# Reordering the gated-delta recurrence and the first tile's output path in a hybrid attention and expert-retrieval kernel

## The chip, the cores and the metric

The kernel runs on one core of a Trainium2 chip. A time is the device time of one execution in microseconds. Three timed runs of the kernel before took 1912.2, 1913.64 and 1914.07 us, with a median of 1913.64.

## What is computed

One decoder layer is applied to 512 prompt tokens and to 8 sample tokens, all in float32. Cut to what matters here, it is:

```python
h = rmsnorm(x, g_pre_mix) * (1 + sc1) + sh1
proj = h @ w_in                    # attention q, k, v; conv input; decay, beta; z; gates g_a, g_b
o_att = sliding_window_attention(q, k, v)
# gated delta rule, in chunks, per head (DK = DV = 128)
tmat = inverse(I + lmat)           # lmat strictly lower triangular in a chunk
u, w = tmat @ (v * beta), tmat @ (k * beta * exp(g))
for each chunk:
    v_new = u_i - w_i @ S
    o     = (q_i * exp(g_i)) @ S + a_i @ v_new
    S     = S * exp(g_last) + (k_i * exp(g_last - g_i)).T @ v_new
o_d = rmsnorm(o, delta_norm) * silu(z)
merged = sigmoid(g_a) * (o_att @ w_att_out) + sigmoid(g_b) * (o_d @ w_delta_out)
x = x + gt1 * rmsnorm(merged @ w_out, g_post_mix)
h2 = rmsnorm(x, g_pre_ffn) * (1 + sc2) + sh2
# expert retrieval, 8 heads: the best 16 of 128 keys on both halves, the best 16 of their 256 sums
f = sum over (head, e) of softmax(best)[e] * gelu(h2 . expert_u[idx[e]]) * expert_v[idx[e]]
x = x + gt2 * rmsnorm(f, g_post_ffn)
```

The new caches and states are outputs too.

## The kernel before

The program is written by hand for five queues: PE (`tensor`), DVE (`vector`), ACT (`scalar`), GpSimd (`gpsimd`) and SP (`sync`, which issues most DMAs). Each runs its instructions in the order in which they are written, and waits on semaphores. Nothing reorders them, so this order is the schedule.

Tokens are tiled by 128: tiles 0 to 3 are the prompt and tile 4 holds the 8 samples. The recurrence is chunked by 128 too, so chunk 0 is tile 0. Four heads side by side make a product of four 128x128 matmuls into one PSUM bank of 512 columns.

The stages are the projections and attention (to about 350 us), the triangular inverse (to about 456 us), the recurrence with tile 0's way to its experts (to about 522 us), and the expert stage (the rest). The inverse is built by doubling: levels 1 to 6 each make, for the four chunks, a first product (`Lm`, `Wc`), copied to `A2` by ACT, and a second product (`A2`, `Tc`), subtracted by DVE. Level 6 writes `Wc`, the transposed inverse, and counts `wt_ready`.

The expert stage makes 520 gathers. GpSimd's `indirect_dma_start` (L446) fetches 128 rows of 8 KB of `euv`, an expert's u and v side by side, into a ring of 7 slots (`SLOTS`). DVE multiplies u with the replicated h2 and sums (L2086), ACT takes gelu and scales a pattern (L800, L804), PE sums the v parts (L1412) and frees the slot. The other tiles' projections, norms, queries and searches are woven between the ticks by tables. Slots 0, 1, 4, 5 and 6 lie over the convolution's outputs `ct`, slot 3 over `Wc`.

PSUM has 8 banks. `dring` (4 banks, `dbank`) goes from PE to DVE and `aring` (2 banks, `abank`) from PE to ACT: `to_fill` waits until a bank was freed, `to_read` until it was filled. `fsum` (2 banks) holds sums in the early and the last stage.

The names in the recurrence are these. On PE, `new_values(ch)` makes the product with `Wc`, `carried(ch)` the state's and the output's products from the new values, `state_products(ch)` the products of the state `delta` with keys and queries, `outputs(ch)` transposes the normed output, `first_deltas(half)` multiplies it with `w_delta_out` for tile 0, `mix(0, e)` makes a quarter (256 columns) of tile 0's `merged @ w_out`, `turned(0)` transposes h2, `first_query` and `first_scores` make the queries and key scores, `select(0)` the gather's indices. `sample_state(h)` with DVE's `state(h)` and `state_sum(h)` updates the samples' states, one head each. On DVE, `asked(ch)` makes the right side of the new values, `decayed(ch)` decays output and state, `carried()` adds what PE made, `squares()` and `normed(ch)` norm the output with ACT's `root_o(ch)`, `gated(ch)` multiplies by the gate; `search(0, piece)` finds the best keys of head 0. ACT's `mixed(0, e)` copies a quarter, `part_squares` sums its squares.

## Time and profile before

| What | Value |
|---|---|
| Median of the three timed runs | 1913.64 us |
| The profiled execution's own time | 1913.76 us |
| Its span | 1911.9 us |
| PE busy | 1452.9 us (76%) |
| DVE busy | 1249.1 us (65%) |
| ACT busy | 674.3 us (35%) |
| GpSimd busy | 620.9 us (32%) |
| DMA, all queues | 645.40 MB, mean 338 GB/s |
| Software queue q0 (the gathers) | 555.82 MB, 70.4% of 16 engines' span |
| Chain that ended last: DMA, PE, DVE, ACT | 39%, 37%, 10%, 6% |

A busy share is a mean over stages with different limits. The page's row of DMA shares is 3 or 4 tenths through most of the first quarter and 9 tenths from the twelfth of 40 slices to the last. In the timelines below, a row has the start in us, the duration in us, the engine, the line, the operation with its output and inputs, the count of instructions run together, and in brackets the idle time before with what ended it. A 128-column product in float32 counts as two PE instructions there, so x8 is one product over four heads. In the windows a pair is busy us with the count in brackets, and PEclk is the granted clock as a share of 2.4 GHz.

### The profile page before, as it was taken

Reading aid. Unit: us, or ns where it says so; the run is one execution under the profiler, and the core shown is the slowest. Engines: PE = TensorE matmul, PEld = TensorE weight load, DVE = VectorE, ACT = ScalarE, POOL = GpSimd, SP = SyncE. Lnnn points to the kernel's source line nnn. Section 1 sums busy time; section 2 is a strip of 40 time slices with the busy share of each in tenths; the row PEclk is TensorE's granted clock in tenths of the full one; section 3 lists DMA queues with packets and bytes.
Section 4 is the critical chain, followed back from the end, with each engine's and each line's share of the span. In section 5 each row is a group of like instructions: output and inputs, shape, how many; then the busy total and the mean of one; then the engine's idle time right before and its main releaser. Section 6 shows DMA issues by size and latency. Waiting matters only on the chain.

```text
span 1911.9 us, 22867 instructions
## 1 busy us (share of the span) xinstructions
PE 1452.9 (76%) x7696; PEld 680.8 (36%) x7696; DVE 1249.1 (65%) x2815; ACT 674.3 (35%) x1745; POOL 620.9 (32%) x590
## 2 busy tenths in 40 slices
PE   9999899999888879587877666666666666666565
PEld 4777678888734446133323111110110110000000
DVE  2077644787576655957767777676776667776765
ACT  3145544411344443723423232342332233322223
POOL 1100000000033424354444544444345444444442
PEclk9999999899999989689888766776676676666766
DMA  9533344103499999999999999999999999999997
GB/s 357 155 126 107 114 132 135 59 32 142 155 367 422 421 410 422 416 384 423 416 421 415 424 424 424 424 424 424 422 422 421 422 415 405 424 424 419 421 422 310
DMA packets 100452, 645.40 MB, mean 338 GB/s; under 512 B 11778, under 2 KB 11930, under 8 KB 32325
## 3 DMA queue, kind: packets, MB, share of 16 engines
q0 software_dynamic: 76912, 555.82, 70.4%
q1 hardware_dynamic: 23232, 88.04, 12.6%
q8 instruction: 61, 1.00, 0.2%
q14 instruction: 55, 0.45, 0.1%
q10 hardware_dynamic: 192, 0.09, 0.0%
HBM read 638.73 MB, written 6.18 MB: 337 GB/s over the span
## 4 chain that ended last, share of the span: by engine, by line
DMA 39%; PE 37%; DVE 10%; ACT 6%; issue 6%; POOL 1%; another core or an unknown queue 1%; DVEq 0%; ACTq 0%; SPq 0%; POOLq 0%
DMA arena<-in_euv,consts 38%; PE abank L831 21%; PE dbank L831 4%; PE dbank L1412 4%; DVE arena L2086 4%; PE fsum L1412 4%; ACT consts L804 1%; PE abank L1323 1%; ACT arena L463 1%; POOL arena L446 1%; ACT small L800 1%; DMA arena<-in_wstream 1%; PE abank L1336 1%; DVE arena L2008 1%
## 5 line engine op out<-in xcount | busy, mean ns | idle before, releaser
L2086 DVE CUSTOM_DVE_ANT_0 arena<-arena 128x1024 f32<-128x1024 f32 x520 | 634.0, 1224 | 408.5 <-DMA arena<-in_euv,consts 402.3
L446 POOL DMA_INDIRECT arena<-in_euv,consts x520 | 589.2, 1133 | 767.0 <-PE fsum L1412 378.3
L831 PE MATMUL abank<-arena 128*128 128x256 f32 (+4 forms) x2400 | 537.4, 383 | 18.5 <-ACT arena L463 9.2
L1412 PE MATMUL dbank<-arena,consts 128*32 128x512 f32 x1024 | 351.3, 860 | 218.5 <-ACT consts L804 217.5
L831 PEld LDWEIGHTS abank<-arena 128*128 128x128 f32 (+1 forms) x2400 | 400.1, 193 | 171.1 <-issue 70.8
L1412 PE MATMUL fsum<-arena,consts 128*32 128x512 f32 x1024 | 298.8, 781 | 182.8 <-ACT consts L804 180.8
L800 ACT ACTIVATE small<-small 128x1 f32<-128x1 f32 x520 | 104.8, 202 | 693.9 <-DVE small L2086 686.9
L1412 PEld LDWEIGHTS dbank<-arena,consts 128*32 128x32 f32 x1024 | 41.6, 126 | 492.3 <-ACT consts L804 482.2
L463 ACT ACTIVATE arena<-abank 128x512 f32<-128x512 f32 (+5 forms) x228 | 111.4, 488 | 288.6 <-PE abank L831 268.2
L1412 PEld LDWEIGHTS fsum<-arena,consts 128*32 128x32 f32 x1024 | 37.9, 120 | 391.4 <-ACT consts L804 375.2
L804 ACT ACTIVATE consts<-arena,small 128x32 f32<-128x32 f32 x520 | 167.1, 321 | 17.3 <-ACT small L800 0.3
L831 PE MATMUL dbank<-arena 128*128 128x128 f32 (+6 forms) x624 | 94.7, 323 | 0.7 <-ACTq L633 0.7
L831 PEld LDWEIGHTS dbank<-arena 128*128 128x128 f32 (+2 forms) x624 | 81.7, 198 | 12.0 <-issue 5.9
L800 ACT ACT_TABLE_LOAD x50 | 64.2, 1283 | 3.6 <-DVE small L2086 2.1
L427 POOL DMA_DIRECT2D out_deltas<-arena x1 | 0.5, 537 | 158.4 <-DVEq L1743 158.4
L1637 DVE RECIPROCAL arena<-arena 128x520 f32<-128x520 f32 x8 | 27.2, 3403 | 37.2 <-ACTq L559 37.2
L463 ACT ACT_TABLE_LOAD x34 | 43.6, 1283 | 7.3 <-PE abank L831 5.2
L1608 DVE COPY arena<-arena 128x24 f32<-128x24 f32 x12 | 2.2, 180 | 64.6 <-ACTq L527 64.4
L2086 DVE DVE_READ_ACCUMULATOR2_ANT small<- 128x1 f32 x520 | 42.8, 82 | 0.0
L713 ACT ACT_TABLE_LOAD x32 | 41.1, 1283 | 1.3
L463 ACT ACTIVATE consts<-abank 128x32 f32<-128x32 f32 (+1 forms) x33 | 6.5, 197 | 96.7 <-PE abank L1323 63.3
L1336 PE MATMUL abank<-arena,consts 128*32 128x512 f32 x256 | 37.0, 636 | 1.2 <-ACT consts L463 1.2
(305 smaller groups left out, 1128.8 us busy)
## 6 DMA issues: line engine op xcount, KB each, us to landing
arena<-in_wstream SPq DMA_DIRECT2D x132, 512.0 KB, 4.6
arena<-in_euv,consts POOLq DMA_INDIRECT x520
arena<-in_wout SPq DMA_DIRECT2D x8, 1024.0 KB, 10.3
arena<-mod SPq DMA_DIRECT2D x7, 512.0 KB, 13.4
arena<-in_x SPq DMA_DIRECT2D x5, 512.0 KB, 7.1
arena<-in_sdel POOLq DMA_DIRECT2D x1, 2048.0 KB, 8.3
out_deltas<-arena POOLq DMA_DIRECT2D x1, 2048.0 KB, 7.5
out_yp<-arena SPq DMA_DIRECT2D x4, 512.0 KB
```

What stands on the lines that cost most here:

```text
L446: pool.indirect_dma_start(ring[n % SLOTS], None, I["euv"], bass.IndirectOffsetOnAxis(cur[:, u % 2, c:c + 1], 0)).then_inc(ring_in[n % SLOT ...
L463: step(A(dst, src, func, **kw), s.aring_free)
L713: A(gexp[r, :], best[r, :], ACT.Exp, bias=nbest[r, :], accum_out=gsum[r, :]).then_inc(s.gexp_ready, 1)
L800: step(A(gel[:, q % 2, place:place + 1], dot[:, q % 2, place:place + 1], ACT.Gelu), s.gelu_done)
L804: A(S[:, q % 2, place, :], E4g[:, u % 2, c0:c0 + 32], ACT.Copy, scale=gel[:, q % 2, place:place + 1]).then_inc(s.diag_ready, 1)
L831: return pe.matmul(out, lhsT, rhs, start=first, stop=last)
L1323: last = pe.matmul(b[32 * k:32 * k + 32, 8 * j:8 * j + 8], ident[:, 32 * j:32 * j + 32], pick[:, :, 4 * k:4 * k + 4], start=True, stop=Tru ...
L1336: last = pe.matmul(b[32 * k:32 * k + 32, :], ident[:, 32 * j:32 * j + 32], h2_all[t][:, g * 512:(g + 1) * 512], start=True, stop=True, ski ...
L1412: last = pe.matmul(out[e][to:to + 32, :], weighed, v, start=h == 0 and kk == 0, stop=h == PH - 1 and kk == 3, skip_group_check=True)
L1637: step(recip(r, r))
L2008: did(0, TT(hit[r], hit[r], bc(sif[r], 2, TOPK), ALU.mult))
L2086: TTR(uh, uh, rep[j] if t < NT else h2sb, 1.0, 0.0, ALU.mult, ALU.add, dot[:, n // NQ % 2, n % NQ:n % NQ + 1]).then_inc(s.dots_done, 1)
```

## The change

The sixth level is taken out of the level loop, in products per chunk, and woven into the recurrence: chunk 0 goes through it first, and the new values of a chunk wait for that chunk's `wt_ready` alone. For chunk 0 the output's product goes to `fsum[0]`, is squared and scaled from there, and its transposition goes to `fsum[1]`; `first_deltas` uses the two `fsum` banks in place of `dring` banks. `state_products` is split in `key_products` and `query_products`. The mix quarters follow each other with less between them, and their weights are requested one by one, each when its place is free, in other places. In the norms the factor rows are multiplied in ahead of the reciprocal root (`gained`, and the products in `first_second`), so that one operation follows it. `warm(3)` makes three products of which nothing is used. The last chunk's recurrence goes behind `search(0, ...)` on DVE and behind `select(0)` on PE; the gather that waits for `o_ready` is now number 3.

PE, from the sixth level of chunk 0 on (`fsum`, `abank`, `dbank` are PSUM banks). Before:

```order
L831 MATMUL abank0<-arena 128x128 x4
L831 MATMUL abank1<-arena 128x128 x4
L831 MATMUL abank0<-arena 128x128 x4
L831 MATMUL abank1<-arena 128x128 x4
L831 MATMUL dbank0<-arena 128x512
L831 MATMUL dbank1<-arena 128x512
L831 MATMUL dbank2<-arena 128x128 x4
L831 MATMUL dbank3<-arena 128x128 x4
L831 MATMUL dbank0<-arena 128x128 x4
L831 MATMUL dbank1<-arena 128x128 x4
L831 MATMUL abank0<-arena 128x128 x4
```

And now, to the transposition of the output:

```order
L840 MATMUL abank0<-arena 128x128 x4
L840 MATMUL abank1<-arena 128x128 x4
L840 MATMUL dbank0<-arena 128x128 x4
L840 MATMUL abank0<-arena 128x128 x4
L840 MATMUL abank1<-arena 128x128 x4
L840 MATMUL abank0<-arena 128x128 x4
L840 MATMUL dbank1<-arena 128x128 x4
L840 MATMUL fsum0<-arena 128x128 x4
L840 MATMUL dbank2<-delta,arena 128x128 x4
L840 MATMUL dbank3<-arena 128x128 x4
L840 MATMUL abank1<-delta,arena 128x128 x4
L1203 MATMUL fsum1<-consts,arena 128x128 x4
```

Chunk 0's new values are the eleventh row before and the fifth now. `sample_state(2)`, the two rows of 512 columns, went behind this stretch.

PE, from the second half of `first_deltas` to the last mix quarter. Before (the first two rows are `carried(1)`, the `delta` rows the state products, L1025 a transposition, the last x4 row `new_values(2)`):

```order
L831 MATMUL dbank1<-arena 128x128 x4
L831 MATMUL dbank2<-arena 128x128 x4
L831 MATMUL dbank3<-arena 128x128 x16
L831 MATMUL dbank0<-delta,arena 128x128 x4
L831 MATMUL abank1<-delta,arena 128x128 x4
L831 MATMUL abank0<-arena 128x256 x8
L831 MATMUL abank1<-arena 128x256 x8
L1025 MATMUL dbank1<-consts,arena 128x128 x4
L831 MATMUL abank0<-arena 128x256 x8
L831 MATMUL abank1<-arena 128x128 x4
L831 MATMUL abank0<-arena 128x256 x8
```

And now (two second products and the new values of chunk 1 first; the rows of 512 columns are `sample_state(3)`):

```order
L840 MATMUL fsum1<-arena 128x128 x16
L840 MATMUL dbank2<-arena 128x128 x4
L840 MATMUL dbank3<-arena 128x128 x4
L840 MATMUL abank0<-arena 128x128 x4
L840 MATMUL abank1<-arena 128x256 x8
L840 MATMUL dbank0<-arena 128x512
L840 MATMUL dbank1<-arena 128x512
L840 MATMUL abank0<-arena 128x256 x8
L840 MATMUL abank1<-arena 128x256 x8
L840 MATMUL dbank2<-arena 128x128 x4
L840 MATMUL dbank3<-arena 128x128 x4
L840 MATMUL abank0<-arena 128x256 x8
```

The state products of chunk 2 and the transposition of output 1 went behind the last quarter.

DVE, ahead of tile 0's first norm (its reciprocal, L1849 before and L1900 now). Before, with `asked(2)`, `gated(1)` and `decayed(2)`:

```order
L1884 TENSOR_TENSOR arena<-dbank,small 128x512
L1885 TENSOR_TENSOR arena<-arena 128x512
L1830 SCALAR_TENSOR_TENSOR arena<-dbank,cols,arena 128x4x128
L1890 TENSOR_TENSOR arena<-arena,small 128x512
L1891 TENSOR_TENSOR delta<-delta,small 128x512
L1849 RECIPROCAL small<-small 128x1
```

And now:

```order
L1912 TENSOR_TENSOR arena<-arena 128x256
L1940 TENSOR_TENSOR arena<-dbank,small 128x512
L1941 TENSOR_TENSOR arena<-arena 128x512
L1912 TENSOR_TENSOR arena<-arena 128x256
L1900 RECIPROCAL small<-small 128x1
L1907 SCALAR_TENSOR_TENSOR arena<-arena,small 128x512 x2
```

`asked(2)` (L1940, L1941) stands between the last two parts of `gained` (L1912), directly ahead of the norm; `gated(1)` and `decayed(2)` went behind both norms.

The diff, cut to its core:

```diff
-                    if n == 4:
+                    if n == 3:
                         pool.wait_ge(s.o_ready, NT)
...
@@ ACT @@
+            first_product(0)
+            first_product(1)
+            first_product(2)
             new_values()
+            first_product(3)
+            act.wait_ge(s.fd_full, 1)
+            step(A(E1[:, 0, :], fsum[0][:, :], ACT.Square), s.psq_ready)
             root_o(0)
             carried_query()
             new_values()
-            root_o(1)
-            carried_query()
...
                 if e == 2:
-                    new_values()
+                    root_o(1)
             root_of(3, parts4[:, 2:3])
+            carried_query()
...
             root_of(5, parts4[:, 4:5])
-            carried_query()
-            root_o(2)
+            new_values()
...
@@ PE @@
+            def warm(times):
+
+                for _ in range(times):
+                    pe.matmul(fsum[0][:, :], ident, consts[:, 0:512], start=True, stop=True)
...
+            first_product(6, 0)
+            first_product(6, 1)
+            second_product(6, 0)
+            first_product(6, 2)
             new_values(0)
+            first_product(6, 3)
             carried(0)
-            sample_state(3)
-            pe.wait_ge(s.wt_ready, NT * 7)
-            state_products(1)
+            key_products(1)
+            second_product(6, 1)
+            query_products(1)
             outputs(0)
+            sample_state(2)
+            first_deltas(0)
+            first_deltas(1)
+            second_product(6, 2)
+            second_product(6, 3)
             new_values(1)
-            first_deltas(0)
-            carried(1)
-            first_deltas(1)
-            state_products(2)
             pe.wait_ge(s.merged0_ready, 1)
             mix(0, 0)
+            sample_state(3)
             mix(0, 1)
+            mix(0, 2)
+            carried(1)
+            mix(0, 3)
+            key_products(2)
+            query_products(2)
             outputs(1)
-            mix(0, 2)
             new_values(2)
-            mix(0, 3)
-            carried(2)
-            state_products(3)
+            warm(3)
...
             turned(0)
+            carried(2)
             pe.wait_ge(s.h2T_ready, 1)
             pe.wait_ge(s.skt_in, 16)
...
+            first_query()
+            first_query()
+            first_scores(0)
+            key_products(3)
+            query_products(3)
+            outputs(2)
+            first_query()
+            first_query()
+            first_scores(1)
+            first_query()
+            first_query()
+            select(0)
+            new_values(3)
+            carried(3)
...
@@ SP @@
-            sp.wait_ge(s.wt_ready, NT * 7)
-            for e in range(3):
-                first_quarter(e)
+            sp.wait_ge(s.lm_ready, NT * 7)
+            first_quarter(0)
             sp.wait_ge(s.mg_ready, NT)
             sp.wait_ge(s.E_ready, NT)
             sp.dma_start(x_t[:, 0, :], I["x"][0:P, :]).then_inc(s.xr0_in, 16)
-            sp.wait_ge(s.sd_ready, 1)
-            for i, v in enumerate(v_first):
-                sp.dma_start(v, bass.AP(tensor=I["mod"].tensor, offset=i * D, ap=[[0, P], [1, D]])).then_inc(s.mod_in, 16)
+            sp.wait_ge(s.a2_ready, NT * 6)
+            first_quarter(1)
+            sp.wait_ge(s.wt_ready, NT * 7)
+            first_quarter(2)
+            sp.dma_start(v_first[0], bass.AP(tensor=I["mod"].tensor, offset=0, ap=[[0, P], [1, D]])).then_inc(s.g1_in, 16)
             sp.wait_ge(s.mx_ready, 1)
             first_quarter(3)
+            sp.wait_ge(s.sd_ready, 1)
+            for i in (1, 2):
+                sp.dma_start(v_first[i], bass.AP(tensor=I["mod"].tensor, offset=i * D, ap=[[0, P], [1, D]])).then_inc(s.mod_in, 16)
...
@@ DVE @@
+            def last_merge(ch):
+
+                b = dring.to_read()
+                step(TT(Wc[:, ch, :], Wc[:, ch, :], b[:, :], ALU.subtract), s.dring_free)
+                dve.sem_inc(s.wt_ready, 1)
...
                 for half in (slice(0, 512), slice(512, D)):
-                    step(STT(h[:, half], h[:, half], rstd[:, 0:1], g1[:, half], ALU.mult, ALU.mult))
-                    step(TT(x_t[:, 0, half], x_t[:, 0, half], h[:, half], ALU.add), s.xs_ready)
+                    step(STT(x_t[:, 0, half], h[:, half], rstd[:, 0:1], x_t[:, 0, half], ALU.mult, ALU.add), s.xs_ready)
+
+            def gained(e):
+                h, g1 = h2_all[0][:, 256 * e:256 * e + 256], v_first[0][:, 256 * e:256 * e + 256]
+                dve.wait_ge(s.psq_ready, e + 2)
+                step(TT(h, h, g1, ALU.mult))
...
+            last_merge(0)
             b = dring.to_read()
             step(copy(delta[:, :], b[:, :]), s.dring_free)
             dve.sem_inc(s.S_ready, 1)
-            b = dring.to_read()
-            step(copy(o, b[:, :]), s.dring_free)
-            squares()
+            dve.wait_ge(s.psq_ready, 1)
+            step(dve.tensor_reduce(rms4, three(R), AX.X, ALU.add), s.o_ready)
+            dve.wait_ge(s.orms_ready, 1)
+            step(recip(rms4, rms4))
+            step(TT(three(o), three(fsum[0][:, :]), bc(rms4, 2, P), ALU.mult), s.on_ready)
+            gated(0)
+            asked(1)
+            last_merge(1)
+            state_sum(2)
+            first_deltas(0)
+            state(3)
+            first_deltas(1)
+            last_merge(2)
+            last_merge(3)
+            decayed(1)
             state_sum(3)
...
             for piece in range(5):
                 search(0, piece)
+            asked(3)
+            gated(2)
+            decayed(3)
             carried()
             squares()
```

## Rows read from the trace of the kernel before

**Rows 1.** Windows: us, busy PE, PEld, DVE, ACT, POOL; PEclk, DMA share, GB/s
```profile
524.00:545.00 21.00, 15.08 (x112) 7.92 (x104) 15.02 (x46) 9.70 (x21) 8.53 (x8) 1.00 1.01 405
545.00:560.00 15.00, 12.61 (x90) 5.47 (x83) 12.06 (x36) 7.19 (x17) 4.64 (x5) 0.89 0.73 251
560.00:1895.00 1335.00, 925.70 (x4348) 271.07 (x4346) 914.54 (x2196) 471.73 (x1371) 587.28 (x539) 0.77 1.01 419
```

**Rows 2.** Timeline of GpSimd: start, us, engine, line, operation, idle before
```profile
522.33 1.03 POOL L446 DMA_INDIRECT arena<-in_euv,consts  x1 [0.28 <-POOL consts L435]
```

**Rows 3.** Timeline of PE, level six to the delta projection
```profile
442.67 2.98 PE L831 MATMUL abank<-arena 128*128 128x128 f32 x24
...
446.98 5.75 PE L831 MATMUL dbank<-arena 8*128 8x512 f32 x36
...
453.29 1.16 PE L831 MATMUL abank<-arena 128*128 128x128 f32 x8 [0.56 <-DVEq L1821]
...
459.07 1.16 PE L831 MATMUL dbank<-delta,arena 128*128 128x128 f32 x8
...
461.95 0.66 PE L1025 MATMUL dbank<-consts,arena 128*128 128x128 f32 x4 [0.83 <-DVE arena L1907]
...
464.40 10.73 PE L831 MATMUL dbank<-arena 128*128 128x128 f32 x80
```

**Rows 4.** Timeline of PE, mixes to select
```profile
476.75 7.12 PE L831 MATMUL abank<-arena 128*128 128x256 f32 x32
...
497.65 1.30 PE L831 MATMUL dbank<-delta,arena 128*128 128x128 f32 x8 [3.75 <-DVEq L1896]
...
504.73 3.24 PE L831 MATMUL abank<-arena 128*128 128x128 f32 x16 [2.30 <-ACTq L692]
...
516.30 4.67 PE L831 MATMUL abank<-arena 128*128 128x128 f32 x40
...
521.03 0.44 PE L1323 MATMUL abank<-arena,consts 128*32 128x8 f32 x32
```

**Rows 5.** Timeline of DVE, level six to the end of the search
```profile
445.18 0.64 DVE L1684 STREAM_TRANSPOSE arena<-arena 32x128 f32<-32x128 f32 x2
...
452.49 3.19 DVE L1820 TENSOR_TENSOR arena<-arena,dbank 128x512 f32<-128x512 f32 x4
...
463.38 0.75 DVE L1830 SCALAR_TENSOR_TENSOR arena<-dbank,cols,arena 128x512 f32<-128x512 f32 x1
...
493.62 0.17 DVE L1849 RECIPROCAL small<-small 128x1 f32<-128x1 f32 x1 [6.88 <-ACT small L653]
...
496.12 0.69 DVE L1857 TENSOR_TENSOR arena<-arena 128x512 f32<-128x512 f32 x1
...
500.90 0.69 DVE L1864 TENSOR_TENSOR arena<-arena 128x512 f32<-128x512 f32 x1
...
512.33 0.49 DVE L1953 MAX8 arena<-arena 128x8 f32<-128x128 f32 x2 [1.09 <-ACTq L776]
...
520.75 0.23 DVE L2018 TENSOR_SCALAR arena<-arena 128x16 f32<-128x16 f32 x1
```

**Rows 6.** Timeline of ACT, same stretch
```profile
454.49 0.60 ACT L463 ACTIVATE arena<-abank 128x512 f32<-128x512 f32 x1 [6.80 <-PE abank L831]
...
459.44 0.30 ACT L637 ACTIVATE small<-small 128x4 f32<-128x4 f32 x1 [4.36 <-DVE small L1902]
...
492.15 0.38 ACT L463 ACTIVATE arena<-abank 128x256 f32<-128x256 f32 x1 [2.32 <-PE abank L831]
```

**Rows 7.** Windows as in rows 1, where the granted clock (PEclk) fell
```profile
465.00:470.00 5.00, 5.00 (x35) 5.00 (x34) 0.82 (x2) 0.23 (x1) 0.00 (x0) 0.72 0.95 330
...
500.00:502.00 2.00, 1.86 (x10) 1.46 (x9) 1.90 (x4) 0.60 (x1) 0.00 (x0) 0.51 0.01 4
...
506.00:508.00 2.00, 2.00 (x12) 2.00 (x11) 0.00 (x0) 0.00 (x0) 0.00 (x0) 0.50 0.04 8
```

**Rows 8.** Issues of DMAs from 440 to 530 us: count, KB, us to landing
```profile
arena<-in_wout SPq DMA_DIRECT2D x4, 1024.0 KB, 8.9
```

194 lines of the change are left out of this document (96 added, 98 removed).

## The prediction

> **What bounds the kernel now.** I read the windows first. From 560 to 1895 us the DMA share is 1.01 and 419 GB/s move, without a break [rows 1]: the 520 gathers of the last stage (L446) keep all DMA engines full. Only their beginning has a hole: 524 to 545 us is full, but 545 to 560 us has a share of 0.73, so 15 x (1.01 - 0.73)/1.01 = 4.2 us are lost there [rows 1]. The bytes are the same after the change, so the end comes as much earlier as the first gather does, and GpSimd's row dates it: 522.33 us [rows 2].
>
> What sets 522.33? I followed it back through the rows of PE, DVE and ACT. Index cast after PE's `select(0)` at 521.03 [rows 4], this after the search of head 0 on DVE (512.33 to 520.98) [rows 5], this after two queries (from 504.73) [rows 4], h2 (DVE, to 501.59), the first norm (from 493.62) [rows 5], the last mix quarter (copied at 492.15) [rows 6], the mixes (from 476.75) [rows 4], the first delta projection (from 464.40), chunk 0's new values (PE, 453.29) [rows 3]. That is the path of token tile 0; whatever else stands in the queues between is filler.
>
> **The change, step by step.** Up to the fifth level's merges nothing is moved, so I start from the same times: first products from 442.67, three in 2.98 us, 0.99 each [rows 3], last transposes on DVE done at 445.82 [rows 5]. Semaphore hops are 0.05 to 0.15 us where nothing stands between (ACT starts 0.04 us after PE's 453.29 + 1.16) [rows 3, 6]. I take 0.1.
>
> 1. *Chunk 0 alone through level six.* Before, the new values wait behind four first products, `sample_state(2)` and four second products (446.98, 5.75 us) and DVE's sums [rows 3]. Now: first products 0 and 1 end at 444.65, second product 0 at 445.65, first product 2 at 446.65. `last_merge(0)`, 0.7 us on DVE after 445.82 (four merges took 3.19 us [rows 5], so 0.7 to 0.8 each), ends at 446.6. New values at 446.75: 6.5 us earlier.
> 2. *Output read from PSUM.* New values 1.0, ACT's copy 0.60 [rows 6], so 448.55; PE is in first product 3 until 448.85; carried key product and output product 2.0 (a group of four 128-column products is 1.0: 1.16 for the first [rows 3]), 450.85; ACT squares 0.6, DVE reduces 0.7, root 0.30 [rows 6], reciprocal and scaling 0.9, transposes 0.66 [rows 3]. `gated(0)` starts at 454.7 instead of 463.38 [rows 5]: 8.65 earlier. It loses a copy and a product on DVE, and `state_sum(3)`, `asked(1)` from in front of it. Reading PSUM from ACT costs what ACT's reading of `abank` costs; I take 0.60, bounds 0.4 and 0.8 (the 128x256 and 128x512 rows are 0.38 and 0.60 [rows 6]).
> 3. *Delta projection.* PE has `sample_state(2)` first (two products of 512 columns, 5.75 less four groups of 1.0 = 1.7), so it starts at 456.25 instead of 464.40 [rows 3]: 8.15. Its last weight block (512 KB) is requested at its first product and needed 5.9 us later. The only row near is twice that size, 8.9 us to landing behind others in the queue [rows 8]; half of it is 4.5 and fits, all of it is 3 too much. I take no wait, bounds 0 and 3.
> 4. *To the last mix quarter.* PE work from there, before: 10.73 (two halves and `carried(1)`), 2 state products, four mixes at 3.56 (two take 7.12 [rows 4]), one transposition, one new-value product; copy at 492.15, 27.75 us after 464.40. After: 7.9 + 3.0 (second products 2, 3, new values 1) + 14.2 + 1.7 (`sample_state(3)`) + 2.0 (`carried(1)`) = 28.8, so the copy is at 485.05: 7.1 earlier. The mixes back to back save nothing; other things left the stretch and these came in. The 1.7 us for DVE's two adds are covered by the 3.0 us on PE.
> 5. *First norm.* Before it started 1.47 us after the copy [rows 5, 6]. Now DVE, in order, stands in front of it with `asked(2)`, whose key product PE makes after the last quarter (486.05), two operations of 0.7, and `gained(3)`, half as wide, 0.4: start at 488.05, not 486.5. This added wait costs 1.5 us. The norm itself drops two of its four operations (a row of 0.69 each; the product by g1 is made in parts while the mixes run): 3.19 us (to 496.81 [rows 5]) become 1.8, x ready at 489.85: 6.95 earlier.
> 6. *Second norm.* Before 4.8 us from x to h2 (501.59 [rows 5]). Now the products by a2 (1.45) run beside ACT's last square (0.6 as a 512-wide copy), read-out and root (0.30) [rows 6], 1.2 in all, then reciprocal and two operations of 0.75: 3.25. h2 at 493.1: 8.5 earlier.
> 7. *Transposition and queries.* `carried(2)` (2.0) is put behind the transposition, so the queries start 2.7 us after h2, at 495.8, before 3.1 (504.73): 8.9. Two queries took 3.24 and 2.0 us, with an output transposition between them [rows 4]; now 2.0 each, because the warming products stand where PE idled for 3.75 us before 497.65 [rows 4]. Scores 0.5, copies 0.8: search at 501.35 against 512.33: 11.0.
> 8. *Select.* DVE's search takes 8.65 us (512.33 to 520.98 [rows 5]) and would end at 510.0, 510.7 with a wait for the exponential, since ACT has the fourth query's and the scores' copies ahead of it. But PE now has state products and outputs (2.6), queries 2 and 3 (4.0), 0.9 for copy and scores, queries 4 and 5 (4.0; with new values 3 they took 4.67 [rows 4]) in front: select at 512.3 instead of 521.03. PE ends last, 8.7 earlier, and the first gather falls at 513.6.
> 9. *Ring.* Gather 3 now waits for the last chunk's squares, which came to stand behind the search: new values, carried, sums end at 518.9, so it goes out 5.4 us after the first, no sooner. Three gathers of 1 MB are 7.5 us of transfer at 419 GB/s, so the engines don't run dry. The first dot product needs the root behind four replication copies; counted in the same way it comes as late after the first gather as before. PE's first products on a gather then come about 0.5 us later than before, since the last output and two queries are served in between; I charge these 0.5 us to the hole.
>
> Sum: -8.7 + 0.5 = -8.2 us. The profiled execution took 1913.76 us (span 1911.9), 0.12 above the median of the three timed runs. 1913.76 - 8.2 = 1905.6 us.
>
> **A rule of the skill.** From 500 to 502 us the granted clock was 0.51, the 1.2 GHz level, and at 506 to 508 still 0.50, after PE's 3.75 us of idleness; at 465 to 470 it was 0.72, a mean of the two levels, after short gaps [rows 4, 7]. In the new order PE has no gap over 0.7 us from 442 to 491 and works through at 2.4 GHz. The Trainium skill's page "TensorE: Matmul & The Clock Gate" says in part 4, on PE-mode transpose, that transposes don't count as PE being busy in the way products do. By it the transpositions behind the warm-up would not keep the clock, and by that rule the queries would be slow as before; no row here tells, since the transpositions before the queries came with the clock already down. What it would do is the first rival below.
>
> **Rivals.**
> - *A cold query stage.* The warm-up ends near 491.2, h2's first half comes at 492.4, and the clock falls anyway. For: the clock was down from 500 to 508 us after such a wait [rows 7]. Against: `carried(2)` now fills in. Price: 1.2 us (one query at 3.24 as before) up to 7.1 (all work to the second scores doubled); at 3.5, 1909.1 us.
> - *A late quarter.* Quarter 2 is requested only when all four merges are done (467.6) and needed at 475.85: 8.3 us, where the median to landing was 8.9 [rows 8]. For: the delta output (2 MB) and x run on the same engines. Against: before, three such quarters were queued at once. A landing a third over that row, 11.8, costs 3.5: 1909.1 us.
> - *Gain given back in the in-order queues*: a second wait like step 5's that I did not see, or half of step 2's: gain 3 to 5, 1909.8 us.
> - *The hole closes.* The 4.2 us at 545 to 560 came with a granted clock of 0.89 [rows 1]. If the ring finds PE free there, all come back: 1901.4 us.
> - *Slower: the clock falls in the dense stretch.* From 460 to 485 us PE runs 25 us of work with no slack. If a short gap at `first_deltas` (its last weight block, step 3) drops the clock as at 465 us [rows 7] and it stays at 1.2 GHz, each us of work costs one more: 25 - 8.2 = 17 us slower, 1930 us. It decides from 8.2 us of halved work on, and from 12 shows as slower. Before, the fall lasted under 5 us with gaps on both sides; now no gap feeds it.
>
> **How the numbers follow.** My forecast 0.60, its own range 1903 to 1908.5; cold queries 0.10, late quarter 0.07, given back 0.10, hole closed 0.08, slower 0.05. Within 0.2% (3.8 us) of the median can't be told from no change. Faster by more: 0.60 + 0.06 + 0.05 + 0.05 + 0.08 = 0.84; same 0.11; slower 0.05. The range goes from 1901.5 (hole closed) to 1910.3 (given back, with the bounds of steps 2 and 3).
>
> **What would show it.** In the rows after: new values 6 to 7 us earlier than 453.29 (step 1); the three-operand multiply of `gated(0)` near 454.7; first norm's reciprocal near 488 with `asked(2)` right before it (step 5); queries of 2.0 us; select released by PE's own queue and not by DVE (step 8); first gather near 513.6; gather 3 held until about 519, and a DMA share of 1 in between (step 9). A first gather at 513.6 with the end less than 5 us earlier would break the reading that the end follows the first gather. A first gather after 518 breaks the sum.

## The result and the profile after

| | Before | After |
|---|---|---|
| Median of six executions each, same chip | 1912.25 us (1906.93 to 1914.07) | 1900.3 us (1897.33 to 1901.7) |
| Ratio of the two, 95% interval | 1 | 0.9939 [0.9926, 0.9952] |
| The profiled execution | 1913.76 us, span 1911.9 | 1901.70 us, span 1899.9 |

In these executions the change makes the kernel faster by 12 us. The forecast was 8.2 us, and its range ended 1.2 us above the measured median.

The windows of the kernel after, with the columns of [rows 1]:

```profile
535.00:540.00 5.00, 2.61 (x16) 1.00 (x9) 4.82 (x13) 4.07 (x10) 1.86 (x2) 0.99 0.91 311
540.00:545.00 5.00, 5.00 (x16) 1.84 (x15) 4.64 (x20) 1.44 (x5) 0.56 (x1) 0.67 0.62 236
545.00:550.00 5.00, 5.00 (x53) 2.57 (x52) 1.23 (x2) 0.50 (x1) 3.37 (x4) 1.00 0.80 267
550.00:560.00 10.00, 9.12 (x36) 3.67 (x34) 7.54 (x22) 4.01 (x15) 4.76 (x6) 1.00 1.01 421
560.00:1895.00 1335.00, 914.34 (x4349) 263.14 (x4348) 916.85 (x2189) 475.25 (x1371) 579.90 (x533) 0.77 1.00 416
```

The long stage is as it was in [rows 1]: the DMA engines are full. The hole is still there too. It begins 10 us sooner, and 5 x (0.10 + 0.39 + 0.21)/1.01 = 3.5 us are lost in it, against 4.2.

GpSimd after, from the first gather on (compare [rows 2]):

```profile
510.94 1.35 POOL L446 DMA_INDIRECT arena<-in_euv,consts  x1 [0.28 <-POOL consts L435]
...
516.53 1.28 POOL L446 DMA_INDIRECT arena<-in_euv,consts  x1 [1.71 <-DVE small L1958]
...
527.74 1.23 POOL L446 DMA_INDIRECT arena<-in_euv,consts  x1 [5.90 <-PE fsum L1454]
```

The first gather is at 510.94 instead of 522.33, 11.4 us earlier, and from there to the span's end it is 1389.0 us instead of 1389.6. That is the whole 12.0. The two other rows are gathers 3 and 7. Gather 3 now waits for DVE's sum over the last chunk's squares, as step 9 said, 5.59 us after the first; gather 7 waits for PE to free a slot.

PE after (compare [rows 3, 4]):

```profile
445.83 3.25 PE L840 MATMUL abank<-arena 128*128 128x128 f32 x24
...
456.28 7.41 PE L840 MATMUL fsum<-arena 128*128 128x128 f32 x64
463.53 1.95 PE L840 MATMUL dbank<-arena 128*128 128x128 f32 x16
...
480.46 3.62 PE L840 MATMUL abank<-arena 128*128 128x256 f32 x16
...
487.57 2.74 PE L1272 MATMUL fsum<-consts 128*128 128x512 f32 x6
491.22 1.44 PE L1034 MATMUL abank<-consts,arena 128*128 128x128 f32 x8 [0.92 <-DVE arena L1920]
492.50 1.95 PE L840 MATMUL dbank<-arena 128*128 128x128 f32 x16
494.29 3.74 PE L840 MATMUL abank<-arena 128*128 128x128 f32 x32
...
505.97 3.74 PE L840 MATMUL abank<-arena 128*128 128x128 f32 x32
509.64 0.44 PE L1363 MATMUL abank<-arena,consts 128*32 128x8 f32 x32
```

The row at 445.83 holds first product 2, the new values and first product 3. The row at 456.28 is the delta projection, 480.46 the last mix quarter, 487.57 the warming products, 494.29 the first two queries, 505.97 queries 4 and 5, and 509.64 the select, which stands right behind them and waits for nothing else. Look at starts, not at durations: 456.28 to 463.53 is 7.25 us although the row says 7.41, and 505.97 to 509.64 is 3.67 us for four groups of four heads, 0.92 each.

DVE after (compare [rows 5]), then ACT (compare [rows 6]):

```profile
446.22 0.69 DVE L1870 TENSOR_TENSOR arena<-arena,dbank 128x512 f32<-128x512 f32 x1
...
454.57 0.75 DVE L1882 SCALAR_TENSOR_TENSOR arena<-fsum,cols,arena 128x512 f32<-128x512 f32 x1 [0.83 <-PE fsum L1203]
...
485.08 0.69 DVE L1940 TENSOR_TENSOR arena<-dbank,small 128x512 f32<-128x512 f32 x1 [0.41 <-PE dbank L840]
...
486.99 0.16 DVE L1900 RECIPROCAL small<-small 128x1 f32<-128x1 f32 x1
487.19 1.54 DVE L1907 SCALAR_TENSOR_TENSOR arena<-arena,small 128x512 f32<-128x512 f32 x2
488.76 1.42 DVE L1917 TENSOR_TENSOR arena<-arena 128x512 f32<-128x512 f32 x2
490.22 0.16 DVE L1900 RECIPROCAL small<-small 128x1 f32<-128x1 f32 x1
490.41 1.54 DVE L1920 SCALAR_TENSOR_TENSOR arena<-arena,small 128x512 f32<-128x512 f32 x2
...
499.78 0.49 DVE L2018 MAX8 arena<-arena 128x8 f32<-128x128 f32 x2 [1.14 <-ACTq L781]
...
508.20 0.23 DVE L2083 TENSOR_SCALAR arena<-arena 128x16 f32<-128x16 f32 x1
```

```profile
448.22 0.60 ACT L463 ACTIVATE arena<-abank 128x512 f32<-128x512 f32 x1 [0.70 <-PE abank L840]
...
451.00 0.60 ACT L648 ACTIVATE arena<-fsum 128x512 f32<-128x512 f32 x1 [1.29 <-PE fsum L840]
...
484.19 0.38 ACT L463 ACTIVATE arena<-abank 128x256 f32<-128x256 f32 x1 [0.98 <-PE abank L840]
```

448.22 copies chunk 0's new values, 451.00 squares its output out of PSUM in the assumed 0.60 us, and 484.19 copies the last quarter. `asked(2)` (485.08) stands ahead of the first norm, as foreseen. The search ends at 508.43 and the select comes at 509.64: PE ends last.

| Milestone | Before | Forecast | Measured |
|---|---|---|---|
| `gated(0)` on DVE | 463.38 | 454.7 | 454.57 |
| First delta product on PE | 464.40 | 456.25 | 456.28 |
| Copy of the last quarter | 492.15 | 485.05 | 484.19 |
| Reciprocal of the first norm | 493.62 | 488.05 | 486.99 |
| h2 | 501.59 | 493.1 | 491.95 |
| Queries | 504.73 | 495.8 | 494.29 |
| Search | 512.33 | 501.35 | 499.78 |
| Select | 521.03 | 512.3 | 509.64 |
| First gather | 522.33 | 513.6 | 510.94 |

Up to the delta projection the forecast holds within 0.15 us. From there the kernel is ahead of it: by 0.9 us at the copy, 1.1 at the norms, 1.5 at the queries, 2.7 at the select. Most of that comes where PE's own work is the path.

### The profile page after: what moved, and what is told of

Same layout as the page of the kernel before. It is cut to its first block, busy times and chain, and to the rows that moved or that the text cites. A ratio compares the mean times of both kernels' runs of the same rounds, so it can differ in the third digit from the quotient of the medians.

```text
span 1899.9 us, 22885 instructions
## 1 busy us (share of the span) xinstructions
PE 1445.7 (76%) x7702; PEld 673.0 (35%) x7702; DVE 1249.1 (66%) x2815; ACT 675.8 (36%) x1746; POOL 619.9 (33%) x590
## 4 chain that ended last, share of the span: by engine, by line
DMA 38%; PE 38%; DVE 8%; ACT 8%; issue 6%; POOL 1%; another core or an unknown queue 1%; ACTq 0%; DVEq 0%; SPq 0%; POOLq 0%
DMA arena<-in_euv,consts 38%; PE abank L840 21%; PE fsum L1454 4%; PE dbank L840 4%; PE dbank L1454 4%; DVE arena L2154 4%; ACT consts L813 2%; ACT arena L463 1%; ACT small L809 1%; POOL arena L446 1%; PE abank L1363 1%; ACT L720 1%; DMA arena<-in_wstream 1%; ACT L809 1%
## 5 line engine op out<-in xcount | busy, mean ns | idle before, releaser
L840 PE MATMUL abank<-arena 128*128 128x256 f32 (+4 forms) x2400 | 529.6, 380 | 12.5 <-ACT arena L463 6.6
L1454 PE MATMUL dbank<-arena,consts 128*32 128x512 f32 x1024 | 355.2, 856 | 220.2 <-ACT consts L813 215.9
L840 PEld LDWEIGHTS abank<-arena 128*128 128x128 f32 (+1 forms) x2400 | 395.1, 190 | 163.2 <-issue 64.9
L840 PE MATMUL dbank<-arena 128*128 128x128 f32 (+5 forms) x552 | 85.4, 325 | 0.7 <-ACTq L636 0.7
L840 PEld LDWEIGHTS dbank<-arena 128*128 128x128 f32 (+1 forms) x552 | 72.2, 194 | 11.6 <-issue 5.6
```

Of the source, the lines that this page charges most:

```text
L840: return pe.matmul(out, lhsT, rhs, start=first, stop=last)
L1454: last = pe.matmul(out[e][to:to + 32, :], weighed, v, start=h == 0 and kk == 0, stop=h == PH - 1 and kk == 3, skip_group_check=True)
```

## The experiments

Stages ahead of the change do not end at the same time in every execution: the last transposes on DVE before level six are done anywhere from 441.4 to 446.2 us in the fourteen profiles of this study. So milestones are compared below from that point on, called t0 (445.82 before, 446.19 after). From t0 the first gather comes after 76.51 us before and 64.75 after. Each kernel below was profiled once, so a difference in milestones is between two single executions.

Wherever a time ratio is given, it is against the kernel before on the same chip, in brackets its 95% interval. The experiments ran on three chips, on which the kernel before had medians of 1907.11 us (31 executions), 1907.74 (30) and 1909.19 (9), so ratios are compared between them and not medians.

**Level six of all chunks first.** The kernel after, with only the order of step 1 put back:

```diff
-            first_product(6, 0)
-            first_product(6, 1)
-            second_product(6, 0)
-            first_product(6, 2)
+            for ch in range(NT):
+                first_product(6, ch)
+            sample_state(2)
+            for ch in range(NT):
+                second_product(6, ch)
             new_values(0)
-            first_product(6, 3)
             carried(0)
             key_products(1)
-            second_product(6, 1)
             query_products(1)
             outputs(0)
-            sample_state(2)
             first_deltas(0)
             first_deltas(1)
-            second_product(6, 2)
-            second_product(6, 3)
             new_values(1)
...
```

> The changed kernel, with the sixth level of all four chunks again ahead of chunk 0's new values, and sample_state(2) ahead of its second products; all else as changed. Theory A (PE's work is what the path waits for up to the last mix quarter; the order within it only decides how much PE idles): chunk 0's new values come 6 us later than at 446.9, but the work that now stands behind them no longer does, so the last quarter's copy (484.19) comes only by the idle time later, 2.5 to 4 us, and so does the first gather (510.94): 513.5 to 515. Theory B (my sum: the lead of chunk 0 is carried on): the copy and the first gather 6 us or more later, 517 or after.

Measured: ratio 0.9989 [0.9975, 1.0003], median 1904.43 us. `gated(0)` comes 14.19 us after t0 instead of 8.38, the first gather 71.01 instead of 64.75. The two numbers are close, 5.8 and 6.3 us, but it is not the same delay carried through. PE begins the delta projection only 4.9 us later (14.99 us after t0 instead of 10.09), since in the kernel after `sample_state(2)` stands in front of it. There the 0.9 us are absorbed. The projection itself then takes 1.6 us longer, because PE's clock is down:

```profile
459.87 9.04 PE L838 MATMUL fsum<-arena 128*128 128x128 f32 x64 [0.93 <-DVE arena L1876]
```

In windows, with the columns of [rows 1]:

```profile
460.00:462.00 2.00, 2.00 (x10) 2.00 (x11) 1.23 (x2) 0.00 (x0) 0.00 (x0) 0.51 0.28 45
462.00:465.00 3.00, 3.00 (x23) 3.00 (x22) 0.00 (x0) 0.00 (x0) 0.00 (x0) 0.76 0.98 377
```

2 x 0.49 + 3 x 0.24 = 1.7 us of full-speed work are lost in these two windows, at the very place where [rows 7] have their first fall. Behind the projection PE waits 1.25 us for DVE about where the kernel after makes two second products (1.8 us), so of the later start only 0.4 us come back. So of the 11.8 us between the first gathers of before and after, the order is worth 6.3 in this execution, and 6.3 - 1.6 = 4.7, an estimate, where the clock doesn't fall. The fall came behind gaps between 452 and 460 us that the kernel after doesn't have. That closing them prevents it is not shown: the kernel before and the one with the new norms alone have such gaps in all three of their profiles, and the fall in one (see below).

**Norms in the old form.**

```diff
-                    step(STT(x_t[:, 0, half], h[:, half], rstd[:, 0:1], x_t[:, 0, half], ALU.mult, ALU.add), s.xs_ready)
+                    step(STT(h[:, half], h[:, half], rstd[:, 0:1], g1[:, half], ALU.mult, ALU.mult))
+                    step(TT(x_t[:, 0, half], x_t[:, 0, half], h[:, half], ALU.add), s.xs_ready)
...
-            gained(0)
-            gained(1)
             carried()
...
```

`gained(2)`, `gained(3)` and the products by a2 ahead of the second root are gone too.

> The changed kernel with both norms as before: four operations in each, none made ahead. From the reciprocal of the first norm to the last part of h2 the changed kernel takes 4.96 us on DVE (486.99 to 491.95). Theory A: 7.1 us as 4 x 0.72 + reciprocal twice, so h2 1.7 us later after gained(3)'s 0.4 is taken off, and the first gather 1.7 later (512.6). Theory B (PE ends last before select, by 1.2 us, and has slack nowhere else): the same, since h2 releases the queries. Rival: the norms don't count because carried(2) or another queue item hides them: 0 to 0.5 us.

Measured: ratio 0.9974 [0.9959, 0.999], median 1902.01. The queries' search comes 55.79 us after t0 instead of 53.59, the first gather 66.95 instead of 64.75: the premultiplied rows are worth 2.2 us.

**The norms' new form alone, in the kernel before.** `gained(0)` to `gained(3)` stand together ahead of `first_normal`.

> The kernel before with the new norms alone: products by the rows ahead of the reciprocal, one operation after it; nothing moved. Theory A: h2 (501.59 before) 1.4 us earlier, since the state's sums stand on DVE between the two norms; the first gather (522.33) 1.4 us earlier if PE's clock behind it is as before. Rival: PE's clock is down then (0.5 from 500 to 508 us before) and eats a part or adds to it: 0 to 3 us earlier.

Measured: ratio 0.999 [0.9978, 1.0003], median 1906.19, first gather 73.54 us after t0, where [rows 2] are 76.51. But only half of these 3.0 us belong to the edit. Up to the last quarter the instructions are the same as before, and its copy came 44.72 us after t0, not 46.33:

```profile
460.00:490.00 30.00, 27.91 (x190) 26.01 (x188) 15.04 (x25) 7.99 (x24) 0.00 (x0) 1.00 0.75 289
...
490.00:492.00 2.00, 1.70 (x11) 1.70 (x12) 1.78 (x4) 0.88 (x3) 0.00 (x0) 0.75 0.95 373
492.00:494.00 2.00, 1.97 (x10) 1.67 (x9) 1.90 (x4) 0.42 (x1) 0.00 (x0) 0.50 0.72 293
```

The clock stayed at 1.00 through the delta projection, where [rows 7] show 0.72 at 465 to 470 us. So the clock fall there, 1.6 us, was part of the one profile of before and not of the kernel. From the copy on, the edit gave 1.4 us: the queries start 11.22 us behind it instead of 12.58. The fall after PE's wait (2.40 us here) was there again, and so was the one in the first queries, which take 3.41 us here and 3.24 in [rows 4].

**No warming products.**

```diff
             new_values(2)
-            warm(3)
```

> The changed kernel without the three warming products. PE is then idle from about 487.6 to 491.2. Theory A (the clock was kept by them): granted clock 0.5 for some us from 491 on, the first two queries 3 us or more instead of 3.74 for both, first gather 1.2 to 4 us later. Theory B (the dense work before was enough, and the transpositions and carried(2) behind): the clock stays at 1.0 and the first gather moves less than 0.3 us.

Measured: ratio 0.9963 [0.9951, 0.9976], median 1900.24; the first gather 66.35 us after t0 instead of 64.75. Without them PE is idle for 3.49 us ahead of the transposition, and the windows of this kernel show what follows:

```profile
490.00:492.00 2.00, 0.75 (x5) 0.51 (x6) 1.86 (x5) 0.73 (x3) 0.00 (x0) 0.98 0.68 274
492.00:494.00 2.00, 2.00 (x10) 2.00 (x11) 1.82 (x3) 1.07 (x2) 0.00 (x0) 0.50 0.01 4
494.00:498.00 4.00, 4.00 (x32) 4.00 (x32) 2.82 (x5) 0.21 (x1) 0.00 (x0) 0.83 0.00 0
```

The same stretch of the kernel after:

```profile
492.00:494.00 2.00, 1.99 (x18) 1.99 (x19) 1.82 (x3) 1.17 (x2) 0.00 (x0) 1.00 0.00 0
494.00:498.00 4.00, 4.00 (x37) 3.83 (x35) 3.28 (x7) 0.57 (x2) 0.00 (x0) 1.00 0.14 28
```

With six matmuls of 512 columns the clock is at its upper level through the transposition, `carried(2)` and the queries. They are worth 1.6 us at the first gather; in the ratios of the times the two kernels can't be told apart. Without them PE also waits longer, so one could lay the fall on the length of the wait. Two other experiments speak against that. With the warming products and waits of 2.40 us (the old norms) and 2.49 (the mix quarters apart) the clock stayed at 1.00, while the norms alone, without them, had 0.50 behind a wait of 2.40. Over all profiles, the clock fell at this place in none of the ten with warming products and in all four without, three of which are the kernel before and its variant.

**A later search.** DVE gets eight unused copies of 512 columns ahead of the first search:

```diff
+            for _ in range(8):
+                step(copy(at(HIT0, 512), h2_all[0][:, 0:512]))
             for piece in range(5):
                 search(0, piece)
```

> The changed kernel with eight copies of 128x512 on DVE ahead of the search, whose results nobody uses: 8 x 0.4 to 0.7 us, 3.5 to 5.8 in all. Theory A (the end follows the first gather one for one): the first gather that much less the 1.2 us that DVE has to spare ahead of select, so 2.3 to 4.6 us later, and the whole time the same amount longer, the hole in the DMA share behind the first gathers unchanged at 3.5 us. Rival (the hole takes up a part of any shift, since the ring's first reuse waits for PE's other work): the time moves by less than half of it.

Measured: ratio 0.9974 [0.996, 0.9987], median 1903.48. The copies moved the search by 2.6 us, the select by only 1.43 (64.88 us after t0), the first gather by 1.73 (66.48), since PE ended 1.2 us after DVE and that slack came first. But in GpSimd's row gather 3 has moved more:

```profile
512.12 1.03 POOL L446 DMA_INDIRECT arena<-in_euv,consts  x1 [0.28 <-POOL consts L435]
...
520.76 1.27 POOL L446 DMA_INDIRECT arena<-in_euv,consts  x1 [5.08 <-DVE small L1958]
```

8.64 us stand between them instead of 5.59, more than the 7.5 us of transfer that cover the wait, and the DMA share from 3 to 13 us after the first gather is 0.93, where the kernel after has 0.99. That is also what holds gather 3: behind waits of 1.36 and 0.93 us around the select, the granted clock is 0.50 from 512 to 518 us, and `carried(3)`, which feeds the squares, takes 3.78 us instead of 2.05. The span is 4.1 us longer than after's with t0 0.55 earlier. Which theory that favours can't be said: the stage behind the first gather, 1391.9 us here, was 1389.0 and 1393.2 in two profiles of the unaltered kernel after.

**The select one query earlier.**

```diff
             first_query()
-            first_query()
             select(0)
             new_values(3)
+            first_query()
             carried(3)
```

> The changed kernel with select(0) between the fifth and the sixth query on PE, and the sixth query behind the new values of chunk 3. Theory A (PE ends last ahead of select, DVE's search is done 1.2 us before, at 508.43 against 509.64): the first gather 1.1 us earlier, 509.8; the fourth gather, which waits for the last chunk's squares, about 0.4 us later, 7.0 us after the first, still inside the 7.5 us that the first three transfers last; the time 1 us shorter, 1899. Rival: the delay of the last chunk opens a gap in the DMA share at 517 to 520, and nothing is gained.

Measured: ratio 0.9957 [0.9944, 0.9969], median 1899.9. The select now waits for DVE's search, as it should, and the first gather comes 63.88 us after t0, 0.87 earlier. In the time 0.9 us can't be seen, as the interval is wider than that, but the ring does not follow:

```profile
509.98 1.03 POOL L446 DMA_INDIRECT arena<-in_euv,consts  x1 [0.28 <-POOL consts L435]
...
516.90 1.27 POOL L446 DMA_INDIRECT arena<-in_euv,consts  x1 [3.35 <-DVE small L1958]
...
528.33 0.95 POOL L446 DMA_INDIRECT arena<-in_euv,consts  x1 [6.12 <-PE fsum L1454]
```

Gather 3 is 6.92 us behind the first instead of 5.59 and gather 7 is 18.35 behind instead of 16.80. In this profile the ring lost what the first gather won: from 3 to 45 us after it 42 x (1.01 - 0.89)/1.01 = 5.0 us of full transfer are missing, against 3.7 in the kernel after.

**The output over SBUF.** Step 2 undone: the output goes to a bank of `dring`, DVE copies and squares it.

```diff
-            step(A(E1[:, 0, :], fsum[0][:, :], ACT.Square), s.psq_ready)
...
+            b = dring.to_read()
+            step(copy(o, b[:, :]), s.dring_free)
+            squares()
+            normed(0)
...
```

> The changed kernel with chunk 0's output again copied to SBUF and squared there by DVE, in place of the square on ACT out of PSUM; the transposition stays in fsum. On the way to gated(0) a copy and a product of 0.72 each replace ACT's 0.6 and its hops (0.2): 0.7 us more. Theory A (PE waits for nothing else there): PE idles 0.7 us ahead of the transposition, and the first gather comes 0.7 us later. Rival: less than 0.3, because other items of PE's queue fill in.

Measured: ratio 0.9964 [0.9948, 0.998], median 1899.78. `gated(0)` 9.13 us after t0 instead of 8.38, the first gather 65.50 instead of 64.75: 0.75 us, one pass of DVE, carried through unchanged, as theory A had it. It can't be seen in the times.

**The mix quarters apart again.** `carried(1)` and the state products of chunk 2 stand ahead of quarter 2, and `outputs(1)` between 2 and 3; on DVE `asked(2)` and `gated(1)` move ahead of the last two parts of `gained`, and on ACT the root for output 1 is taken one quarter earlier.

```diff
             mix(0, 1)
-            mix(0, 2)
             carried(1)
-            mix(0, 3)
             key_products(2)
             query_products(2)
+            mix(0, 2)
             outputs(1)
+            mix(0, 3)
```

> The changed kernel with the state products of chunk 2 and the transposition of output 1 back between the mix quarters (carried(1) and the state products ahead of quarter 2, the transposition ahead of quarter 3). They are 0.9 + 0.9 + 0.45 = 2.3 us of PE. Theory A: the last quarter's copy 2.3 us later, but asked(2) is then done before it and the first norm starts 1.3 us after the copy in place of 2.8, so the first gather comes 0.8 us later. Rival (my step 4: being back to back saves nothing): below 0.3 us. Rival the other way: the full 2.3 us.

Measured: ratio 0.9972 [0.996, 0.9984], median 1901.77. The copy of the last quarter is 2.49 us later (40.49 us after t0), the first gather 1.32 (66.07). `asked(2)` is done by then, so the norm starts 1.57 us behind the copy and not 2.80, which gives half of it back, between theory A's 0.8 and the full 2.3. PE then waits for h2:

```profile
485.44 2.74 PE L1272 MATMUL fsum<-consts 128*128 128x512 f32 x6
490.67 1.44 PE L1034 MATMUL abank<-consts,arena 128*128 128x128 f32 x8 [2.49 <-DVE arena L1920]
```

After such a wait of 2.49 us, with the warming products before it, the clock was still 1.00.

**The pair again, and an earlier first dot.** Two questions were left: how large the gain is in another set of runs, and whether the hole closes when DVE makes the first dot products ahead of the last chunk's norm. In `early_dots` that norm goes behind the first tick, in `early_both` the select is one query earlier too.

```diff
             gate_pattern(0)
-            normed(NT - 1)
...
                 if i == 0:
+                    normed(NT - 1)
                     gated(NT - 1)
```

> The changed kernel, unaltered, beside the next two on one chip. The kernel before had a median of 1907 us over 61 later runs, 5 us below the first ones. Theory A (that kernel's first profiled run was one of its slower executions: stages ahead of the change end between 441.4 and 446.2 us in the nine traces, and its clock fell at 465 us): the changed kernel is again near 1900, and the gain is 7 to 8 us. Rival: the changed kernel is lower too, near 1896, and the gain of 12 us stands.

> The kernel before, unaltered, once more with a profile. Theory A: counted from the end of the fifth level's transpositions on DVE (445.82 in the first trace) the last mix quarter is copied after 44.7 us if the clock stays up at 465 us, as in norms_alone, whose program is the same up to there, or after 46.3 if it falls; the first gather follows 30.2 us later in either case.

> The changed kernel with the last chunk's scaling on DVE (normed(3), which waits 3.1 us for ACT's root at 517 to 520 us) behind the first two dot products in place of ahead of them. Theory C (the end follows the ring's reuse by DVE and PE more than the first gather: end less start of gather 7 spreads over 2.4 us in nine traces, end less first gather over 4.0): first gather unmoved, DVE's later work 2.4 us earlier, the hole in the DMA share behind the first gathers 1 to 2.4 us smaller, time 1 to 2.4 us shorter. Theory A (the end follows the first gather alone): no change.

> early_select and early_dots together. early_select had its first gather 0.9 us earlier and no shorter time. Theory C: no gain over early_dots, since the ring's reuse, not the first gather, is what the end follows. Theory A: 0.9 us shorter than early_dots.

Measured:

| Kernel | Median, us | Ratio | First gather from t0 | Gather 7 from the first |
|---|---|---|---|---|
| after again | 1902.04 | 0.9959 [0.9945, 0.9974] | 66.38 | 17.09 |
| before again (one execution) | 1908.44 | | 73.49 | 16.22 |
| `early_dots` | 1900.99 | 0.9954 [0.994, 0.9967] | 64.74 | 17.07 |
| `early_both` | 1901.88 | 0.9957 [0.9944, 0.9971] | 63.90 | 18.34 |

The gain is 7.8 us by the ratio here, 7.2 by the medians (1909.19 for before, nine executions), not 12. The two profiles say where 4 us can go. Before, again:

```profile
459.00:462.00 3.00, 2.21 (x19) 1.97 (x19) 2.75 (x5) 0.50 (x1) 0.00 (x0) 1.00 1.04 437
462.00:465.00 3.00, 3.00 (x30) 3.00 (x29) 0.60 (x1) 0.09 (x1) 0.00 (x0) 1.00 0.91 289
...
492.00:494.00 2.00, 0.84 (x4) 0.84 (x5) 1.78 (x4) 1.02 (x3) 0.00 (x0) 0.54 1.02 404
```

This is the same program as in [rows 7], t0 3.1 us earlier, and the fall at the delta projection is missing, as with the norms alone. The last quarter's copy comes 44.95 us after t0 instead of 46.33, and from the second norm's reciprocal to the search it takes 12.29 us instead of 13.93, since the fall in the first two queries is missing as well:

```profile
500.24 2.05 PE L831 MATMUL abank<-arena 128*128 128x128 f32 x16 [1.38 <-ACTq L692]
```

[rows 4] have 3.24 us there. The first gather is 3.0 us sooner, 28.54 us behind the copy where 30.2 was expected, with no instruction changed. That is why this unaltered kernel is as early as the one with the new norms (73.49 and 73.54). And after, again, has this on PE:

```profile
481.98 3.72 PE L840 MATMUL abank<-arena 128*128 128x256 f32 x16 [1.38 <-DMA arena<-in_wout]
```

The last quarter's weights were late, and the copy came at 39.63 us after t0 instead of 38.00. This is the rival of the late quarter, in a mild form: 1.6 us. The four requests of `w_out` took a median of 9.5 us to landing here, and 6.6 in the first profile of the kernel after.

The earlier dot products were made 4.2 us sooner after the first gather (5.96 us behind it instead of 10.11), and gather 7 came no sooner. Its slot is freed by a product that waits for ACT, and ACT's row shows why that did not move:

```profile
523.15 1.28 ACT L809 ACT_TABLE_LOAD   x1 [0.16 <-ACT arena L463]
524.44 0.20 ACT L809 ACTIVATE small<-small 128x1 f32<-128x1 f32 x1
```

In order, gelu stands behind the copies of the last queries, and these behind PE: it comes 15.12 us behind the first gather, and 14.30 and 15.14 in the two profiles of the kernel after. So theory C's gain did not come: 4.6 us of full transfer are missing from 3 to 45 us after the first gather, against 3.7 and 3.3. That the end follows the ring's reuse is neither shown nor ruled out by it. No version is measurably better than the kernel after.

## Why the prediction was wrong

The path was right from step to step. What failed is the size of PE's terms in steps 4, 7 and 8, too long by 2.4 us together, and the baseline, whose rows held clock falls that not every execution has.

- **Steps 1, 2 and 3 held.** `gated(0)` and the delta projection are within 0.15 us of the forecast, from a start 0.37 later. The square from PSUM took 0.60. The last weight block was in time. The experiment on level six shows that most of the lead of chunk 0 reaches the first gather: 5.8 us at `gated(0)` are 4.9 at the projection and, without the clock fall, about 4.7 at the gather.
- **Step 4 failed, by 0.9 us: "PE work from there ... 28.8".** It was 27.9. I added durations from rows, 1.0 for a group of four products and 7.9 for the delta projection. A row's duration has the modelled tail of its last matmul in it, and a sum of rows pays it every time. Between starts the delta projection is 7.25, and the second products and new values are 2.7 and not 3.0. The rows had it: [rows 4] give 4.67 us for 40 records, 0.93 for a group of eight with one tail in five, and I wrote 1.0 in the same sentence.
- **"The mixes back to back save nothing" was wrong too.** Apart they cost 2.5 us at the copy and 1.3 at the first gather. The sum of step 4 had this right, as it leaves `outputs(1)` and the state products out; the sentence beside it was wrong. I had looked at PE's total alone. What stands behind the last quarter doesn't delay it, and the order decides what does.
- **Step 5 held:** `asked(2)` and `gained(3)` delay the norm, 2.80 us from the copy against the 3.0 of the forecast. Step 6 is right to 0.1. By the two runs on the norms their new form is worth 2.2 us behind the change and 1.4 in the kernel before at an equal clock.
- **Steps 7 and 8 failed by 0.4 and 1.1 us, for the same reason as step 4:** `carried(2)` is 1.79 between starts (492.50 to 494.29) and a query 1.84 (3.67 for two from 505.97 on), not 2.0. The mechanism of step 8 was right: PE ends last, and the earlier select shows it (0.87 us to be had until DVE's search is the wait).
- **Step 9 was half right.** Gather 3 is held 5.6 us, and the share stays at 0.99. I charged 0.5 us to the hole, and it lost 0.7 less than before. That the whole time then moved by the first gather's 11.4 and 0.6 more is partly luck: the stage behind the first gather took from 1387.9 to 1396.1 us in the fourteen profiles, and in the second pair it was 2.8 us longer after than before. "The end comes as much earlier as the first gather does" is too simple: with the earlier select the ring's loss grew by 1.3 us where the first gather won 0.9, and with the later search it grew too.
- **The baseline.** Of the 76.51 us from t0 to the first gather, 3.0 are clock falls: the one in the delta projection, which two other profiles of the same instructions don't have, and the one in the first queries, which one of the two doesn't have. The kernel after has no fall there, so in that pair of profiles it wins them; in the second pair it doesn't. Since I worked out the times of after at the upper clock and set them against rows of before that hold the falls [rows 7], these 3.0 us were in my 8.7, and I never asked whether each execution has them. The start was high too: I took 8.2 from 1913.76, and the median of before's six executions was 1912.25.

Sum for the profiled pair: -8.7 forecast at the first gather, -2.7 from steps that were sized too long (PE's pitch: 0.9 in step 4, 0.4 in step 7, 1.1 in step 8, the rest DVE's in steps 5 and 6), -0.6 behind it: -12.0. From t0 the same working gives 67.8 us to the first gather (513.6 - 445.82), against 73.49 in the second profile of before: -5.7, and 3.0 from the steps that were too long. The second pair has 73.49 - 66.38 = 7.1 with the late weights and would have 8.7 without them.

The rivals: no cold query stage. The clock was 1.00 from 492 to 498 us, with transpositions right behind the warming products; the rule in part 4 of the Trainium skill's page "TensorE: Matmul & The Clock Gate", that transposes don't count as busy, is not contradicted, since 1.44 us of them are all there is between the warming products and `carried(2)`; no run here has a stretch of them long enough to test it. The late quarter occurred in one of two profiles of the kernel after, and in none of the nine variants of it. The hole did not close (3.5 us). The clock did not fall in the dense stretch: 1.00 from 440 to 525 us.

What stays open: how often the kernel before has each clock fall, and so whether 12 or 8 us is the typical gain (the ratios are 0.9939 and 0.9959, and their intervals overlap). The 70 later executions of the kernel before, with medians of 1907.11, 1907.74 and 1909.19 against 1912.25 for the first six, speak for 8. Open is also what decides whether a wait takes the clock down, and why the stage behind the first gather took 1389.0 us in one profile of the kernel after and 1393.2 in the other, with the same instructions.

## What to carry to other kernels

Count work on a path from start to start of rows, not by adding durations, and take the pitch from the longest row of the same kind. Before a baseline's rows become terms of a sum, look at the granted clock beneath them and price the fall apart, because another execution may not have it. A feeding stage in front of a saturated one pays as long as the transfers already issued cover the wait for the ring's next slot. That from there on its other producers have to come earlier too is argued here and not shown: making the first dot products earlier brought no slot forward.

## What the runs showed of the hardware

- Products of 128x128 by 128 columns in float32 start every 0.11 us at the upper clock (64 in 7.25 us), and a group of eight records (four heads) every 0.89 us; the row of a group alone reads 1.06 to 1.16.
- A gap of 2.49 us on PE behind six warming matmuls of 512 columns (2.74 us) left the granted clock at 1.00, and one of 3.49 us without them took it to 0.50 for the next 2 us and 0.83 for the 4 after. The length of the gap alone did not decide: one of 2.40 us was followed by 0.50 in one kernel (the norms alone) and by 1.00 in another (the old norms, with the warming matmuls), and gaps of 1.36 and 0.93 us close together by 0.50 for 6 us (the later search).
- The same program on PE had a granted clock of 0.72 for 5 us in the delta projection in one execution and of 1.00 there in two others, 1.6 us of difference. The first two queries took 3.24 us in one execution of the kernel before and 2.05 in another.
- ACT's square of 128x512 from PSUM takes 0.60 us, as its copy does.
- Weights of 1 MB that had arrived in time in one execution kept PE waiting for 1.38 us in another of the same kernel.
